# Moves of q between two attention tiles, issued by ScalarE's queue instead of SyncE's

## What is computed

```python
h = rms_norm(x, norm_gain)
proj = einsum('bsd,de->bse', h, w_in)        # pool_v, pool_g, q, k, v, attn_g, 512 columns each
y_pool = multiscale_pool(pool_v, pool_w, pool_scale) * silu(pool_g)
# 8 heads of 64; chunks of 64 queries, each reads its own chunk and the 8 before it
s = einsum('bhqd,bhkd->bhqk', q, k) / 8 + rel_bias[clip(key - query, -64, 64)]
y_attn = softmax(s) @ v * silu(attn_g)
x = x + concatenate([y_pool, y_attn]) @ w_out
out = rms_norm(x, final_norm_gain)
```

## Time and profile before

| | us |
|---|---|
| median of 3 runs | 1804.39 |
| lowest and highest | 1802.91, 1806.52 |
| the profiled execution | 1807.24 |
| its span (first to last instruction) | 1805.3 |

### The profile page before, as it was taken

The page is one execution under the profiler, slowest core; times in us unless marked ns, Lnnn a source line. Parts: engine busy times, 40 slices in busy tenths (PEclk is TensorE's granted clock), DMA queues, the critical chain, the costliest instruction groups (busy, mean ns, idle before and its releaser), DMA issues. The chain is left out here.

```text
span 1805.3 us, 43433 instructions
## 1 busy us (share of the span) xinstructions
PE 1653.8 (92%) x17680; PEld 1205.3 (67%) x17680; DVE 1065.5 (59%) x2182; ACT 841.6 (47%) x1580; POOL 710.5 (39%) x740
## 2 busy tenths in 40 slices
PE   4999999999895999999779999999999999999977
PEld 1554554478573767776568777777777887778754
DVE  6778768656453556544255655666556665566655
ACT  4555555412111112111046665675657766567664
POOL 6545536201111212000423545554456644456443
PEclk8999999999996999999999999999999999999989
DMA  5565555552452542443843334433344233442332
GB/s 198 199 221 184 192 199 201 194 184 97 161 189 104 187 152 83 160 167 108 226 138 110 100 111 144 130 107 105 102 147 133 104 113 106 136 147 93 104 94 82
DMA packets 148093, 257.81 MB, mean 143 GB/s; under 512 B 11928, under 2 KB 73896, under 8 KB 145848
## 3 DMA queue, kind: packets, MB, share of 16 engines
q1 hardware_dynamic: 146856, 253.73, 42.1%
q0 software_dynamic: 1040, 1.31, 0.4%
HBM read 151.33 MB, written 83.48 MB: 130 GB/s over the span
## 5 line engine op out<-in xcount | busy, mean ns | idle before, releaser
L2022 POOL TENSOR_TENSOR stages<-stages 128x512 f16<-128x512 f32 (+1 forms) x368 | 367.4, 1014 | 444.7 <-ACT stages L1805 442.2
L1474 PE MATMUL bank<-middle,weights 128*128 128x128 f16 x1792 | 314.7, 220 | 0.6 <-DVE middle L1511 0.5
L1477 PE MATMUL bank<-middle,weights 128*128 128x128 f16 x1792 | 314.3, 220 | 0.0
L1476 PE MATMUL bank<-middle,weights 128*128 128x128 f16 x1792 | 314.2, 220 | 0.0
L1892 DVE CUSTOM_DVE_ANT_0 stages<-bank,stages 128x640 bf16<-128x640 f32 (+4 forms) x256 | 199.8, 780 | 151.4 <-PE bank L1635 149.2
L1799 ACT ACTIVATE stages<-bank,log_ps 128x512 f32<-128x512 f32 (+1 forms) x368 | 222.0, 603 | 132.7 <-POOL stages L2022 46.0
L963 PE MATMUL bank<-middle 128*128 128x256 f16 x784 | 216.3, 276 | 27.3 <-ACT stages L1016 18.9
L966 PE MATMUL bank<-middle 128*128 128x256 f16 x784 | 216.4, 276 | 0.0
L965 PE MATMUL bank<-middle 128*128 128x256 f16 x784 | 216.3, 276 | 0.0
L1805 ACT ACTIVATE stages<-stages 128x512 f16<-128x512 f32 (+1 forms) x368 | 202.9, 551 | 11.7
L986 PE MATMUL bank<-entry,stages 128*128 128x512 f16 x768 | 174.3, 384 | 19.0 <-DVE entry L1184 19.0
(11 more groups left out here) (147 smaller groups left out, 3545.4 us busy)
## 6 DMA issues: line engine op xcount, KB each, us to landing
entry<-in_x SPq DMA_DIRECT2D x64, 512.0 KB, 3.6
h_ops<-middle SPq DMA_DIRECT2D x16, 1792.0 KB, 6.3
middle<-h_ops SPq DMA_DIRECT2D x112, 256.0 KB, 5.2
middle<-h_ops SPq DMA_DIRECT2D x49, 512.0 KB, 7.8
middle<-middle SPq DMA_DIRECT2D x192, 128.0 KB, 2.5
residual<-entry SPq DMA_DIRECT2D x32, 512.0 KB, 2.8
entry<-residual SPq DMA_DIRECT2D x30, 512.0 KB, 4.1
out<-entry SPq DMA_DIRECT2D x30, 512.0 KB, 2.9
```

Source lines behind the costliest of these rows:

```text
L1474: nc.tensor.matmul(dst, wh, hop3[:, o, 0, kt, :], start=(kt == 0 and s < 2 and pair == 0), stop=False, skip_group_check=True)
L1476: nc.tensor.matmul(dst, wh, hop3[:, o, 1, kt, :], start=False, stop=False, skip_group_check=True)
L1477: mm = nc.tensor.matmul(dst, wl, hop3[:, o, 0, kt, :], start=False, stop=(kt == 3), skip_group_check=True)
L2022: nc.gpsimd.tensor_tensor(p_l[:, h % 2, c + a:c + b], p32[:, s, a:b], p_h[:, h % 2, c + a:c + b], ALU.subtract).then_inc(A["pl_done"], 1)
```

## The change

`move_q(sp, t)` leaves SP's round; `move_q(act, t)` stands at the head of ACT's boundary, ahead of `branch_hi`. The two waits of `move_q` and its six DMAs go with it. `move_q(sp, 0)`, at the end of the q stage, stays on SP.

```diff
@@ -1820,6 +1820,7 @@
 
             def boundary(t):
                 if t > 0:
+                    move_q(act, t)
                     for j in range(2):
                         branch_hi(t - 1, j)
                 if t < LAST:
@@ -2066,7 +2067,6 @@
                     sp.wait_ge(A["wob_lo"], NKT)
                 else:
                     move_k(sp, t)
-                    move_q(sp, t)
                     load_v(sp, t)
                     load_gate(sp, t)
                 if t == LAST:
```

## The result

The changed kernel is slower: 1869.77 us median (1865.88 to 1871.88, 4 runs) against 1803.87 (1802.91 to 1806.52, 4 runs). The ratio is 1.0353, its 95% interval 1.0335 to 1.0371. The forecast was 1817.1, slower, with a range up to 1829: the direction was right, the size wrong by a factor of five.

What follows compares the result with a forecast made beforehand. TensorE, busy 92%, was taken to bound the kernel; q landing 1.0 us later was to cost 8.0 us at 8 boundaries, 3.75 at 5 and 1.0 at the last, together 12.75, giving 1817.1 us, range 1798 to 1829.

Steps and rivals of the forecast that it cites:

- check (3): Sign in the changed profile: PE waits on L1635 at 13 or 14 boundaries, about 19 us in all instead of 6.7.
- Is there room for both?: At tile boundaries, two queues were to raise the rate of moves from 191 GB/s by 1.3 to 1.7.
- the prediction's own sum: Per boundary: 2.42 us of k alone, remaining moves, 3.1 of loads, 1.8 start and landing; q taken as 1.0 us later.
- the prediction's own count of boundaries: PE pays the full delay at 8 boundaries, the delay less 0.25 us at 5, the full delay at the last.
- Much slower, one generator for both queues: Rival: ACT's and SPq's issues exclude each other and alternate, q lands 2.0 us later; 26.8 us slower, 1831; chance 0.12.
- Faster: q overtakes: Rival: at boundaries q lands by S+8.6, ahead of the loads; 5.4 us faster, 1799.0; chance 0.25.
- They take turns packet by packet, whatever the size: On the DMA engines, queues alternate single packets, so the four times larger loads get through before q's moves are done.
- The range: 1798 to 1829 us, from the faster rival's 1799 past the forecast's 1827, leaving out most of the much slower one.

Runs made afterwards that it cites:

- e1: The changed kernel, but SyncE waits until all six moves of q have landed before issuing the loads of v and the gates; 1801.74 us, ratio 0.9987.
- e3: The kernel before, all on SyncE's queue, but in the order k, v, gates, q; 1880.03 us, ratio 1.0413.
- e6: e1 with q's and k's six moves each reordered so that consecutive ones read the other half of nat's partitions; 1803.59 us, ratio 0.9984.
- e7: The changed kernel, with 56 needless 128 x 128 products on PE ahead of its waits for the moves; 1861.76 us, ratio 1.0301.
- e5: The changed kernel, but SyncE waits for q's moves before loading the gates; v's loads go out as in the change; 1831.87 us, ratio 1.0135.
- e4: e1, and ScalarE also waits until k's moves have landed before it issues q's; 1836.96 us, ratio 1.0175.

## Why the prediction was wrong

**Right.** The place (the first `maxima` of each tile), the mechanism (v's and the gates' loads come forward into q's window), the side, and that ScalarE's issues fit: they end at S+7.2 and L1775 starts on time. The forecast's check (3), waits at nearly all boundaries, came true, with 57.1 us where it had 19.

**The step that failed: "Is there room for both?"** It took 191 GB/s at a share of 0.86 as issue-bound and gave the moves 253 to 330 GB/s once two queues pile them up, and the loads 343 on top. e1 and e3 show piled-up moves at 193 and 198 GB/s, at shares of 1.22 and 1.14, and the batch as a whole at 215 in every order. The 253 of the earlier trace rows came from one stretch of the first tile. Rates near it do occur, but not for long: 249 in e1 in a stretch of 2.2 us while k's and q's moves run from two queues, 224 in e6. The loads ran at 282 and not 343. With 193 and 282 the prediction's own sum gives 2.42 + 1.11 MB / 193 (5.8) + 1.05 MB / 282 (3.7) + 1.8 = S+13.7, 3.7 us later than before; PE started at S+14.25. By the prediction's own count of boundaries that is 8 x 3.7 + 5 x 3.45 + 3.7 = 50.6 us, and the waits grew by 50.4; that the two agree so closely is in part luck, for the count leaves out the first boundary, which waited 6.2.

A nearer row was there: the last of the earlier trace rows, with two queues at work (one of them a software queue), has 214 GB/s at a share of 1.17. The prediction used its share and not its rate. With it, 2.42 + 2.16 MB / 214 (10.1) + 1.8 = S+14.3.

**The term that was missing: PE's clock.** Nothing in the sum let a longer wait make the products behind it slower. The added waits for k and q are 57.1 - 6.7 = 50.4 us; the busy time of PE grew by 18.2 us, all in the attention stage. e7 takes the slow stretches away and gains 9 us net of its own cost; e5, whose waits stay at 2.6 us or less but for one, loses only 24.4 us.

**The rivals.** "Much slower, one generator for both queues" had the sign and came nearer with 1831, but for a wrong reason: in e4 ScalarE's issue takes 0.642 us, in the change its issues overlap with SyncE's (1424.48 to 1429.59 and 1422.41 to 1426.38), and L1775 isn't late. The Trainium skill, "Perfetto Trace Analysis", section "DMA Instruction — HWDGE", has the generator locked by one sequencer at a time. Issues of 0.62 and 0.82 us that run side by side don't take turns of 0.62 each, which is what the rival needed. That a shorter part of an issue is exclusive stays possible: ScalarE's 0.82 beside SyncE's issues against 0.64 alone would fit it, and cost nothing here. "Faster: q overtakes" did not happen beside the loads; even without them (e1) q gains only enough for 0.13%: its moves alone stay at 193 GB/s.

**The turns.** "They take turns packet by packet, whatever the size" is not borne out. In the changed kernel, with S = 1422.41, q's moves (q10) and the loads (q1) are both on their way from 1430 to 1432 and from 1432 to 1434 us (packets, MB, share of 16 engines):

```profile
q1 hardware_dynamic: 183, 0.33, 77.3%
q10 hardware_dynamic: 297, 0.14, 33.0%
...
q1 hardware_dynamic: 163, 0.29, 64.2%
q10 hardware_dynamic: 429, 0.21, 48.4%
```

q's small packets go 1.6 and 2.6 times as often as the loads' large ones. The loads' bytes still went nearly all ahead of q's last, as the forecast had it, and e3, which has no turns at all, loses at least as much.

**The range.** 1829 as its upper end left no room for either error. The other page cited, "DMA: Bandwidth & Descriptors", section "Issuing engines are not separate DMA queues", of the Trainium skill, says that a second issuing engine saves only the sequencer's time. That held for the kernel's time: the second queue by itself was worth 0.1% (e1). For 2.2 us in e1 two queues did reach 249 GB/s against one queue's 191, but q's last move landed only 0.2 us earlier on average over 13 boundaries.

## What to carry to other kernels

A DMA that leaves a queue also moves up everything that stood behind it. Before moving one, ask what comes forward and whether its bytes then run ahead of something that is waited for; the order on one queue may be the only thing that keeps the bulk loads out of the way. If they must be on separate queues, hold them back by the semaphore of what matters (one wait gave back 66 us here). Before counting on spare room, look at the bytes that such a batch moved and not at the share of the DMA engines. And price a wait of PE with the work behind it: with waits of 3.6 us on average PE's busy time was 18.3 us longer here, with waits of 2.1 us (e5) it was 1.7 us longer.

## What the runs showed of the hardware that was not expected

- SBUF-to-SBUF moves of 64 partitions in 512-byte pieces ran at 191 GB/s at a DMA share of 0.86 and at 193 at 1.22 (e1). The share rose with the number in flight and the rate did not. In another order of the halves (e6) it was 224 at 1.07.
- k's and q's moves and the loads, 2.62 MB, took the same 12.3 us at 215 GB/s in three orders (before, change, e3), at shares of 0.84, 0.98 and 0.91.
- Packets of two hardware queues did not go one for one: 297 of 512 bytes beside 183 that were mostly of 2 KB in 2 us (change).
- Behind PE's waits in the change (3.6 us on average) the granted clock was half (1.2 GHz) for 3.4 us or more at 12 of 13 boundaries; behind those of about 2 us in e5 and e4 at 4 of 26. Products into a bank that nobody reads held it up (e7).
- ScalarE's DMA issue began at 1424.48, 0.36 us before the copy ahead of it on that engine was over (1424.84): here the issues didn't wait for the arithmetic in front of them to end.
- A 16 KB load of instructions ran in q's way at nine of 13 boundaries, and q was late at those alone (before and e1). That it is the cause was not tested.
